# Two models on one core: six banks in the feed-forward, and where the context's steps stand in the first model's heads

## The reference, cut to what matters

```python
def swiglu(h, w_gate_up, w_down):
    gu = h @ w_gate_up
    gate, up = jnp.split(gu, [D_FF], axis=-1)      # D_FF = 2816
    return (jax.nn.silu(gate) * up) @ w_down

def one(args):                                     # _peer, per block of 128 tokens
    hh, ee, gg = args
    a = jnp.einsum("tkd,td->tk", peer_down[ee], hh)
    act = (gg * jax.nn.gelu(a)).astype(hh.dtype)
    return jnp.einsum("tk,tkd->td", act, peer_up[ee])
```

## Time and profile before

| | us |
|---|---|
| median of 3 runs | 4190.04 (4188.73 to 4191.44) |
| the profiled execution | 4178.77 |
| its span, first to last instruction | 4177.5 |
| PE busy | 3664.8 (88%) |
| DVE busy | 2318.4 (55%) |
| ACT busy | 656.9 (16%) |
| POOL busy | 1291.4 (31%) |
| mean granted PE clock | 0.951 |

### The profile page before, as it was taken

How to read it: one execution, slowest core, us unless ns; L and a number is a source line. 1 busy time by engine, 2 the same in 40 slices (tenths; PEclk the granted TensorE clock), 3 DMA queues, 4 the chain that set the end, 5 groups by cost and what they waited for, 6 DMA issues and landing times. The chain is left out here.

```text
span 4177.5 us, 41027 instructions
## 1 busy us (share of the span) xinstructions
PE 3664.8 (88%) x14584; PEld 2586.0 (62%) x14584; DVE 2318.4 (55%) x5464; ACT 656.9 (16%) x1800; POOL 1291.4 (31%) x1125
## 2 busy tenths in 40 slices
PE   8988999998998889999897998777778998887777
PEld 6667788887846778888745874333334786433333
DVE  3432011557757896766742147766764126777875
ACT  2332001110001320000012111111112211111111
POOL 1100000000655566765620014434442002444442
PEclk9999999999999999999999999988999999999989
DMA  8742344334998889998961449988996237999998
GB/s 320 283 193 88 122 151 181 122 130 150 411 390 308 296 334 397 404 392 343 413 238 53 145 186 389 412 340 359 415 416 281 102 116 295 385 419 420 419 419 332
DMA packets 207818, 1208.65 MB, mean 289 GB/s; under 512 B 23696, under 2 KB 24848, under 8 KB 96000
## 3 DMA queue, kind: packets, MB, share of 16 engines
q0 software_dynamic: 154368, 855.71, 51.1%
q1 hardware_dynamic: 53248, 350.32, 22.1%
HBM read 1204.79 MB, written 1.15 MB: 289 GB/s over the span
## 5 line engine op out<-in xcount | busy, mean ns | idle before, releaser
L1298 PE MATMUL bank<-big 128*128 128x256 f32 (+5 forms) x9848 | 2140.5, 378 | 64.1 <-DVE big L1796 8.7
L1298 PEld LDWEIGHTS bank<-big 128*128 128x128 f32 (+2 forms) x9848 | 1833.9, 191 | 377.9 <-issue 72.5
L2489 POOL DMA_INDIRECT big<-in_pboth,big x1024 | 1227.9, 1199 | 1208.1 <-PE bank L1685 705.2
L1685 PE MATMUL bank<-big 128*128 128x512 f32 x2048 | 1000.0, 647 | 276.6 <-ACT big L2453 276.6
L2169 DVE CUSTOM_DVE_ANT_0 big<-big 128x1024 f32<-128x1024 f32 x768 | 926.1, 1223 | 326.0 <-DMA big<-in_pboth,big 323.1
L1685 PEld LDWEIGHTS bank<-big 128*128 128x128 f32 x2048 | 413.4, 207 | 854.3 <-issue 492.6
L2476 POOL TENSOR_TENSOR big<-big 128x1 f32<-128x1 f32 (+1 forms) x49 | 37.7, 770 | 1519.8 <-DVE big L1739 1519.8
L2180 DVE SCALAR_TENSOR_TENSOR big<-big 128x1024 f32<-128x1024 f32 x254 | 326.2, 1284 | 61.5 <-DMA big<-in_pboth,big 41.5
L2453 ACT ACTIVATE big<-big 128x128 f32<-128x128 f32 x512 | 164.9, 391 | 244.0 <-DVE big L2148 239.7
L1333 PE MATMUL bank<-big 128*128 128x128 f32 x596 | 94.9, 294 | 66.0 <-ACT big L2402 19.8
L2443 ACT ACTIVATE big<-big 128x4 f32<-128x4 f32 (+2 forms) x134 | 27.7, 207 | 727.5 <-DVE big L2144 727.4
(11 more groups left out here) (203 smaller groups left out, 2177.0 us busy)
## 6 DMA issues: line engine op xcount, KB each, us to landing
big<-in_w SPq DMA_DIRECT2D x104, 1024.0 KB, 7.6
big<-in_wmod POOLq DMA_DIRECT2D x48, 1024.0 KB, 8.4
big<-in_wgu SPq DMA_DIRECT2D x44, 1024.0 KB, 8.0
big<-in_wzg SPq DMA_DIRECT2D x36, 1024.0 KB, 4.7
big<-in_wro SPq DMA_DIRECT2D x32, 1024.0 KB, 6.9
big<-in_wpq SPq DMA_DIRECT2D x24, 1024.0 KB, 6.1
big<-in_wd SPq DMA_DIRECT2D x22, 1024.0 KB, 8.1
big<-in_pboth,big POOLq DMA_INDIRECT x1024, 11.7
```

The costliest lines, as they stand in the source:

```text
L1298: last = pe.matmul(o, a, b, start=(i == 0), stop=(i == n - 1))
L1685: last = pe.matmul(u.ap, d.ap, row[:, 512 * i:512 * i + 512], start=(k == 0), stop=(k == 127))
L2489: g.indirect_dma_start(out=s.ap, out_offset=None, in_=table, in_offset=bass.IndirectOffsetOnAxis(ap=index, axis=0)).then_inc(s.full[0], 16)
```

## The change

Four edits:

1. **Six banks.** `ffn_in` takes banks from `six` (`pa`, `pa2`, `py`: 0, 1, 4, 5, 2, 3) instead of four; `ffn_out` number i waits for the inner channels that it reads (`acts[2 * i + 1]`) instead of all waiting at the first for the last; `ffn_last` waits for its own three.
2. **Time sums sooner.** `dt_sums` and `group_mask` of the first group stand behind the two conv chunks instead of behind the two gate chunks as well.
3. **Heads.** Between the chunks and pairs of a group the yields were 5.8 each (40.6 for a group) and are now 3.5, 5, none, 6, 7, 5, 7 (33.5); the second step of `group_end` (the turning) stands ahead of the pair of i = 1 instead of behind it. The first four conv chunks and the first two of group 0 yield 4 instead of 7.
4. **Second merge.** The last four output products yield 1 instead of the last two.

The lines of the changed kernel are 9 or 10 higher than those of before behind `ffn_out`.

```diff
--- before.py
+++ after.py
@@ -366,7 +366,7 @@
                 w, u = chunk()
                 BC.append(conv(u, 2 * i, qk[:, 2 * i:2 * i + 2, :], None))
                 put("conv_in", ws=[w], hT=hT, conv=BC[i], ready=None if i else hT_ok)
-                yield
+                yield 4
             BC_ok = BC[3]["done"]
             if l == 0:
                 put("block_consts", rmask=rmask, rope=rope)
@@ -513,10 +513,14 @@
                 yield 2
 
             gots = [{"turn": []} for _ in range(8)]
-            yield from group_inputs(0, gots[0])
+            inputs = group_inputs(0, gots[0])
+            for _ in range(2):
+                next(inputs)
+                yield 4
             dts_ok = tick("dt_summed")
             put("dt_sums", u=self.pa2.take(), dts=dts, ready=la_ok, done=dts_ok)
             group_mask(0)
+            yield from inputs
             pairs = group_heads(0, gots[0])
             next(pairs)
             for g in range(4):
@@ -524,13 +528,17 @@
                 end = group_end(g - 1, gots[g - 1]) if g else iter(())
                 for i in range(4):
                     next(nxt)
-                    yield 5.8
+                    if i == 1:
+                        next(end, None)
+                    else:
+                        yield 7 if i else 3.5
                     next(pairs)
+                    if i == 0:
+                        next(end, None)
                     if i == 2 and g < 3:
                         group_mask(g + 1, gots[g]["cb_read"])
                     if i < 3:
-                        next(end, None)
-                        yield 5.8
+                        yield 6 if i == 1 else 5
                 next(nxt, None)
                 group_gate(g, gots[g])
                 yield 2.5
@@ -567,7 +575,7 @@
                             c.free(self.mt_ok)
                         put("branch_out", ws=[w], u=u, YT=YT, ready=y_ok if n == 0 else [], sig=s.ap[:, m, :], s_ok=s_ok,
                             MT=MT[:, n, :], c=c, done=self.mt_ok)
-                        yield 7.2 if first or n < 6 else 1
+                        yield 7.2 if first or n < 4 else 1
                     s.free(u.free)
 
             yield from merge(True, y_ok, group_end(3, gots[3]))
@@ -608,31 +616,32 @@
             yield 27
 
             fr = Ring([wa[2], wt[0], wt[1], wa[0], wa[1]])
+            six, acts = Banks(self.pa.banks + self.pa2.banks + self.py.banks), []
             for i in range(22):
-                w, u, c = self.load(fr, t["wgu"][l, i], 2048), wide.take(), tmp.take()
+                w, u, c = self.load(fr, t["wgu"][l, i], 2048), six.take(), tmp.take()
                 w.free(u.full)
                 c.free(u.free)
                 put("ffn_in", ws=[w], u=u, hT=hT, c=c, dst=area[:, i, :], tanh=tick("ffn_tanh"),
                     ready=None if i else hT_ok)
-                act_ok = u.free
+                acts.append(u.free)
                 yield
             if l:
                 fw_ok = tick("d_fnorm", 16)
                 put("load_row", dst=fw, src=t["fnorm"][0].to_broadcast([P, 1024]), done=fw_ok, before=[self.x_ok])
-            us = [wide.take() for _ in range(4)]
+            us = [six.take() for _ in range(4)]
             for i in range(8):
                 w = self.load(fr, t["wd"][l, i], 2048)
                 done = tick("ffn_part")
                 w.free(done)
-                put("ffn_out", ws=[w], us=us, act=area, i=i, ready=None if i else act_ok, done=done)
+                put("ffn_out", ws=[w], us=us, act=area, i=i, ready=acts[2 * i + 1], done=done)
                 yield
             ws = [self.load(fr, t["wd"][l, i], 2048) for i in range(8, 11)]
-            put("ffn_last", ws=ws, three=ws, us=us[0:2], act=area, tt=0)
+            put("ffn_last", ws=ws, three=ws, us=us[0:2], act=area, tt=0, ready=acts[17::2])
             put("ffn_add", us=us[0:2], X=X[:, 0, :])
             self.x_ok0 = us[1].free
             r0 = stats(0, late)
             yield 10
-            put("ffn_last", three=ws, us=us[2:4], act=area, tt=1)
+            put("ffn_last", three=ws, us=us[2:4], act=area, tt=1, ready=acts[17::2])
             for w in ws:
                 w.free(us[3].full)
             if l == 0:
@@ -1477,8 +1486,8 @@
 
     def ffn_out(ws, us, act, i, ready, done):
         wk = by2(ws[0].dst)
-        if ready:
-            pe.wait_ge(*ready)
+        pe.wait_ge(*ready)
+        if i == 0:
             for u in us:
                 opened(u)
         pe.wait_ge(*ws[0].full)
@@ -1489,9 +1498,10 @@
                                      start=(i + k == 0), stop=False)
         last.then_inc(done[0], 1)
 
-    def ffn_last(three, us, act, tt, **_):
+    def ffn_last(three, us, act, tt, ready, **_):
         for i, w in enumerate(three):
             wk = by2(w.dst)
+            pe.wait_ge(*ready[i])
             pe.wait_ge(*w.full)
             for k in range(2):
                 for n, u in enumerate(us):
```

## The result

The changed kernel took 4210.2 us (median of 6 runs), the kernel before 4189.2 us beside it: ratio 1.0047, 95% interval 1.0036 to 1.0059. The forecast was no change, 4190. The time lies inside the range (4160 to 4215), but 21 us more is past the 8.4 us that the prediction takes as no change: the kernel became slower. The profiled executions, 4208.6 and 4178.8 us, stand 29.8 us apart.

What follows compares the result with a forecast made beforehand. DVE was taken to pace the second layer's heads, and a chain of small waiting steps the second model's attention. Terms -27 - 12 + 4 - 8 + 0 + 43 = 0 gave no change, 4190 us, range 4160 to 4215.

Steps and rivals of the forecast that it cites:

- the context's tail: Second model's attention layer: 49 `up` and `peer_add` moved there from the heads cost 43 us more, bounds 15 to 50.
- its last line: At the fifth score: last `up` and `peer_add`, 4.7 us waiting and 4.7 work against some 6 of wait, cost 5 us.
- My upper bound of 50: Tail in second model's attention: 50 us at most, with low clock after PE's longer waits and longer powers on POOL.
- Second layer's heads: Second layer's heads: lighter DVE load takes 36 us off, 9 given back, 27 us less; bounds 18 to 40.
- Second feed-forward: Second layer's first output product: the 11.2 us wait goes and `ffn_add` is late next, 12 us less; bounds 0 to 13.
- third rival: Both feed-forwards run at the gathers' pace, so the six banks only move the wait: 4212 us, chance 0.15.
- First feed-forward: First feed-forward: six heads' ranking falls into it and gathered rows come later, 4 us more; bounds 14 more, 8 less.
- the wait of 5 to 10 us near chunk 15: Sign in the first feed-forward: a PE wait of 5 to 10 us near chunk 15, another at the first product.
- the first model's last product: Sign at the first model's end: its last product ends about 43 us earlier, near 2122 instead of 2165.
- Around `mix_out`: First `mix_out`: last four merge output products carry no ranking, waits of 5.4 and 2.0 us go, 8 us less; bounds 3 to 10.
- First layer: First layer's heads and merge: no change, 0 us, with the context's own chain covered by output products; bounds 8 more, 6 less.
- Rows land too slowly: Rival for the tail: rows at 1.9 us instead of 1.37, 49 rows cost 26 us more, 4216 us; chance 0.12.

Runs made afterwards that it cites:

- the leaner run: Changed kernel with context held until the token gates, indices' load later, 0.7 of context pace in second layer's heads, 1.5 times beside gates: 4170.1 us, ratio 0.9962.
- the kernel with banks alone: Kernel before with only the feed-forward edits (six banks, waits moved to each output product): 4167.3 us, ratio 0.9976.
- the two leaner runs: The leaner run (4170.1 us), and the same with the load of `peer_add`'s row issued from POOL's queue instead of SP's (4177.7 us, ratio 0.9979).
- the late sums: Changed kernel with time sums and first group's mask put back behind all four chunks of the first group: 4215.8 us, ratio 1.0057.
- banks with `peer_add` late: Kernel before with six banks and the second model's `peer_add` put behind some of the attention's heads: 4177.7 us, ratio 0.9966.
- the dealing alone: Changed kernel with the feed-forwards' banks and waits as before: 4226.7 us, ratio 1.0128.

## Why the prediction was wrong

It failed in the term for the context's tail, and there in its last line: "the last `up` and `peer_add` ... against some 6 us of wait at the fifth score: 5". Up to the Fourier product my list gave 37.5 us, and 38.8 were measured. That line cost 16.3 us instead: a wait of 5.7 us and eight heads at half clock behind it. The sum priced the wait and gave the clock nothing. My upper bound of 50 allowed 7.5 us for "a low clock after PE's longer waits" and longer powers together; the term came to 55. This is shown by the two pairs of runs that differ in the place of `peer_add` alone (+16.3 to -0.9, and +14.1 to +0.2).

The 38.8 us are in part a lucky hit: the 37.5 were DVE's time only, and by the trace PE's waits grew by 33.5 us there and the slower clock took 5.4 more, which my list had not.

Point by point, the rest, from the table:

- *Second layer's heads*, -23 for -27, inside 18 to 40. DVE's load sets them, as said; the leaner run shows it again. The earlier sums are worth 6 us by themselves, and I had them inside DVE's load.
- *Second feed-forward*, -13 for -12. Right in size, but for a reason I had not seen: with the context on its old schedule 11.7 us of it come back. I looked for what was late next in `ffn_add`; it was the weights behind `peer_add`'s load. In my third rival's words "the wait moves", which is what it did in the kernel with banks alone.
- *First feed-forward*, about -1 for +4. The working held: first gathered row 99 us behind the stage's begin (forecast 94), the add at 1251.3 - 1011 = 240 (241). PE waited 3.0 and 14.8 us, nearly the 18.3 that, in my words, "don't go". But the wait of 5 to 10 us near chunk 15 that I named as a sign did not come, and the first model's last product ended at 2131, 34 us earlier than before, not 43.
- *Around `mix_out`*, -3.2 to -4.8 for -8: the edit that I credited does nothing for it.
- *First layer*, +5 for 0. The heads gained 14 us and the stage behind them lost 19. I had left out SP's queue: the context's `load_iota` waits 22 us for DVE and holds `in_w`, 8.9 us of PE's wait and 1.6 of clock. The run with that load later took 7 us of the 19 away. Most of the rest looks like the context's own chain, whose waits moved out of the heads instead of being covered in the merge: PE's wait for the context's last modulation vectors was 3.2 us among the heads (L1932) and is 3.5 behind them (L1942). No run tests that.
- *Rivals.* "Rows land too slowly" was not it: 49 `up` took 63.0 us with 4.4 us of idle time before them, 1.38 us each, at a DMA share of 0.74:

```profile
L2190 DVE SCALAR_TENSOR_TENSOR big<-big 128x1024 f32<-128x1024 f32 x49 | 63.0, 1286 | 4.4
```

The misses of the terms add up: tail +12, first layer +5, `mix_out` +5, heads +4, first feed-forward -4.5, second -1, together +20.4, nearly the whole of the 21.0 us between the medians.

## What to carry to other kernels

A dealt side stream should be put where the main stream is one long piece of PE's work, and kept out of a chain of short dependent steps: there 49 rows, 67 us of DVE's time, and `peer_add` cost 55 us. Look for the one instruction in the side stream that waits for a load whose buffer it has just freed: it blocks its own engine, and the load blocks every load behind it in SP's queue, up to 50 us here. A wait of 4 us of PE has to be priced with what the clock does until the next dense matmuls, here some three times the wait in all.

## What the runs showed of the hardware

In the waits of 4.1 and 5.7 us PE's granted clock went to half (1.2 instead of 2.4 GHz) and stayed there for 37 to 44 us, through eight heads of 4.8 us in which PE was busy 9.0 to 9.6 of every 10 us. With waits of 1.0 to 1.2 us a head the same instructions mostly stayed at full clock, at 3.5 us a head and 7.3 busy us in 10; in the two leaner runs the clock fell there without a longer wait, for 14 us. In three orders (the changed kernel, the late sums, banks with `peer_add` late) the half clock lasted until `pool`'s denser matmuls; in the dealing alone, behind a wait of 5.2 us, it ended after four heads.

The Trainium skill, TensorE: Matmul & The Clock Gate, in the section on the HAM clock gate, calls it a throttle that activity releases; by that alone the clock would have come back among the heads. The trace disagrees: through those eight heads it did not, and why is open.

The powers on POOL beside the dealt rows took 1.09, 0.72 and 1.72 us, where 0.55 to 0.70 us was read without rows; the cost sits inside the 38.8 us:

```profile
2135.16 0.55 POOL L2486 TENSOR_TENSOR big<-big 128x1 f32<-128x1 f32 x1 [1.99 <-DVE big L1749]
2144.84 1.09 POOL L2486 TENSOR_TENSOR big<-big 128x1 f32<-128x1 f32 x1
2160.74 0.72 POOL L2486 TENSOR_TENSOR big<-big 128x2 f32<-128x2 f32 x1 [7.23 <-DVE big L1749]
2172.91 1.72 POOL L2486 TENSOR_TENSOR big<-big 128x2 f32<-128x2 f32 x1 [1.93 <-DVE big L1749]
```

And full DMA engines alone cost PE nothing: in the second feed-forward's products they stood at 1.00, 399 GB/s, while PE waited for nothing at all.
